# Seven products that nobody reads in the opening of a two-layer hybrid encoder

## The reference

```python
for l in range(DEPTH):
    mod = c_act @ w_ada[l] + b_ada[l]
    x = _layer(x, mod, ...)
...
shift, scale, gate = jnp.split(mod, 3, axis=-1)
h = _rmsnorm(x, norm_w) * (1.0 + scale[:, None]) + shift[:, None]
proj = h @ w_in
```

## Time and profile before

| what | before |
|---|---|
| median of 3 runs | 1139.76 us (1139.59 to 1139.95) |
| the profiled execution | 1139.91 us |
| its span, first to last instruction | 1138.2 us |
| mean granted TensorE clock in the span | 0.993 |
| TensorE busy | 1116.9 us, 98% of the span |
| DVE, ACT, POOL busy | 666.4, 529.3, 569.4 us |

### The profile page before, as it was taken

The page is one execution under the profiler, slowest core; times in us unless marked ns, Lnnn a source line. Parts: engine busy times, 40 slices in busy tenths (PEclk is TensorE's granted clock), DMA queues, the critical chain, the costliest instruction groups (busy, mean ns, idle before and its releaser), DMA issues.

```text
span 1138.2 us, 15271 instructions
## 1 busy us (share of the span) xinstructions
PE 1116.9 (98%) x5843; PEld 920.5 (81%) x5843; DVE 666.4 (59%) x824; ACT 529.3 (47%) x924; POOL 569.4 (50%) x411
## 2 busy tenths in 40 slices
PE   6999999999999999999999999999999999999997
PEld 5778888888888888888898788888788887788885
DVE  4716466579887555538870635665988854131365
ACT  5544266655445524224462535656545453232234
POOL 5536444445535545545814363444445535454455
PEclk8999999999999999999999999999999999999998
DMA  9656423235443456653304463224433523443332
GB/s 322 205 131 204 126 80 88 76 110 139 121 117 73 135 172 199 211 152 104 99 20 102 144 200 93 75 75 120 120 111 94 139 64 84 111 139 93 101 104 93
DMA packets 203482, 140.80 MB, mean 124 GB/s; under 512 B 12001, under 2 KB 191249, under 8 KB 203409
## 3 DMA queue, kind: packets, MB, share of 16 engines
q1 hardware_dynamic: 202632, 138.91, 42.3%
q10 hardware_dynamic: 776, 0.91, 0.3%
HBM read 136.64 MB, written 2.63 MB: 122 GB/s over the span
## 4 chain that ended last, share of the span: by engine, by line
PE 91%; POOL 3%; DVE 2%; SPq 1%; DMA 1%; ACT 1%; issue 0%; DVEq 0%; POOLq 0%
PE main L679 74%; PE psC L679 6%; PE psA L679 5%; PE psB L679 4%; POOL w_lo L597 3%; SPq L395 1%; DMA big<-in_w_ada 1%; PE psB L912 1%; PE psB L892 1%; DVE h_lo L1540 1%; SPq L423 0%; ACT w_hi L1092 0%; DVE psC L1493 0%; DVE tmp L1535 0%; PE psC L921 0%
## 5 line engine op out<-in xcount | busy, mean ns | idle before, releaser
L597 POOL TENSOR_TENSOR w_lo<-raw,w_hi 128x512 fp32r<-128x512 f32 x344 | 510.1, 1504 | 535.6 <-ACT w_hi L1092 535.4
L679 PE MATMUL main<-h_hi,w_hi 128*128 128x512 f32 x976 | 390.4, 401 | 3.8 <-ACT h_hi L1092 2.9
L679 PE MATMUL main<-h_hi,w_lo 128*128 128x512 f32 x976 | 380.0, 390 | 0.0
L679 PE MATMUL main<-h_lo,w_hi 128*128 128x512 f32 x976 | 379.5, 390 | 0.0
L1092 ACT ACTIVATE w_hi<-raw 128x512 fp32r<-128x512 f32 x344 | 200.0, 623 | 309.7 <-PE main L679 174.4
L679 PEld LDWEIGHTS main<-h_hi,w_hi 128*128 128x128 f32 x976 | 183.6, 188 | 52.1 <-issue 11.6
L679 PEld LDWEIGHTS main<-h_hi,w_lo 128*128 128x128 f32 x976 | 183.2, 188 | 39.2
L679 PEld LDWEIGHTS main<-h_lo,w_hi 128*128 128x128 f32 x976 | 183.4, 188 | 37.7 <-issue 1.9
L1855 DVE TENSOR_TENSOR tmp<-main,misc 128x512 f32<-128x512 f32 x32 | 22.1, 691 | 165.6 <-PE main L679 163.1
L1701 DVE SCALAR_TENSOR_TENSOR misc<-main,cols,misc 128x511 f32<-128x511 f32 (+2 forms) x96 | 71.9, 749 | 61.0 <-ACT misc L1092 58.4
L679 PE MATMUL main<-y_hi,w_hi 128*128 128x512 f32 x256 | 100.6, 393 | 0.0
(11 more groups left out here) (282 smaller groups left out, 1418.0 us busy)
## 6 DMA issues: line engine op xcount, KB each, us to landing
raw<-in_w_in SPq DMA_DIRECT2D x124, 512.0 KB, 3.9
xbc<-in_w_ada SPq DMA_DIRECT2D x16, 512.0 KB, 4.8
zs<-in_w_ada SPq DMA_DIRECT2D x16, 512.0 KB, 4.6
raw<-in_w_pc SPq DMA_DIRECT2D x16, 512.0 KB, 3.8
raw<-in_w_out SPq DMA_DIRECT2D x16, 512.0 KB, 3.6
zs<-in_w_ada SPq DMA_DIRECT2D x16, 256.0 KB, 7.7
xbc<-in_w_in SPq DMA_DIRECT2D x8, 512.0 KB, 7.4
big<-in_w_ada SPq DMA_DIRECT2D x16, 256.0 KB, 7.2
```

Source lines behind the costliest of these rows:

```text
L597: nc.gpsimd.tensor_tensor(lo_b[:, cut, :], raw_b[:, cut, :], hi_b[:, cut, :].bitcast(F32), ALU.subtract).then_inc(s_split[b], 2 * BT_ // kt)
L679: return nc.tensor.matmul(o, a, b_, start=start, stop=stop)
```

## The change

Seven products are added to TensorE's stream in the opening. Each multiplies the identity (128x128, fp32) with 256 columns of the transposed rows, and writes columns 512 to 767 of `psB`, where nobody reads them. Three stand between `spread` and the first sums, four between these sums and `wide_pair(0)`. The wait for ACT's copies moves ahead of the first three.

```diff
             spread(psC0, rms, 1)
+
+            def unread(n):
+
+                for _ in range(n):
+                    mm(psB[:, 512:768], ident[:, :], stage_x[:, 0, 0:256])
+
+            pe.wait_ge(s_xca, 2)
+            unread(3)
             quarter_sums(0)
             pe.wait_ge(s_cols, 1)
             pe.wait_ge(s_xc, 2)
-            pe.wait_ge(s_xca, 2)
+            unread(4)
             for q in range(QUARTERS - 1):
                 wide_pair(q)
```

## The result

The changed kernel takes 1141.5 us (median of 21 runs, 1140.61 to 1142.72), the kernel before 1139.75 us (21 runs, 1139.41 to 1140.46). The ratio is 1.0015 with a 95% interval of [1.0009, 1.0022]: 1.75 us slower, which is under 0.2% and clear of zero. It lies within the forecast range, close to its upper end (1141.6), and twice as far from the kernel before as the 0.8 us that I gave.

The account below looks back on a forecast made before the run. DVE was taken to bound the opening, so TensorE's 2.9 us gain brings 0; slow sums of quarter 1 add 0.8 us to the median 1139.76, giving 1140.6, stated as 1140.5. The range was 1139.4 to 1141.6.

Parts of the forecast that it names:

- What bounds the opening: Up to `wide_end`: slab transfers of quarter 1, then DVE set the end, with about 0.1 us to spare over TensorE.
- the 2.9 us of TensorE: First sums and `wide_pair(0)`: full clock frees 0.8 and 2.1 us on TensorE, but gains 0 on the path.
- The clock of the start: Opening: clock 1.00 up to 15.8, then 1.2 GHz until 26.05; first transposes, 0.21 us each, taken at about half speed.
- Price of the products: Added products of 256 columns: 0.45 us each, 1.35 for three and 1.8 for four, twice that at 1.2 GHz.
- Two pauses of 1.8 us: TensorE waits 1.8 us ahead of block 0's low rows and 1.8 more ahead of the sums of quarter 1.
- The clock falls in the pauses: Ahead of the sums of quarter 1: they take 1.87 us, not 1.05, making DVE and all behind it 0.8 late.
- a term that I had put at 0: Low clock reaching beyond the start of `wide_pair(1)`: costs half its length less 0.1 us; likeliest 0.
- Sum: Whole kernel: 0 if the clock holds at 30.9, +0.8 us if not, added to the median 1139.76.
- Faster: Rival in the opening: TensorE, not DVE, holds it and the 2.9 us come through, 1136.9; chance 0.02.
- no effect: Rival in the opening: clock holds at 30.9 or falls where it did, everything covered, 1139.7 to 1139.9; chance 0.37.
- products too long: Rival around the first sums: clock stays low all through, up to +1.1 us, 1140.9; chance 0.06.
- Slower by more than 0.2%: Rival at `wide_pair(1)`: low clock for 4.4 us costs 2.2, slow sums 0.8 more, up to 1142.7; chance 0.07.

Follow-up runs that it names:

- exchanged kernels: One weight load issued ahead of a `w_ada` slab instead of behind it: kernel before 1139.29 us, changed kernel 1139.49, with only the four later unread products 1139.46.
- six zero products: Kernel before plus six products of zero weights directly ahead of `wide_end`, order of loads as before: 1143.32 us, 3.12 +- 0.18 over the kernel before.
- second trace: The changed kernel run again with nothing altered: median 1141.74 us, ratio 1.0015 to the kernel before; the traced execution took 1142.97 us.
- filled kernels: Changed kernel plus three zero-weight products ahead of the sums of quarter 1: 1141.71 us; the same with the weight load ahead of the slab: 1141.03 us.

## Why the prediction was right, and where it was short

The number was right in part by luck. The range held the result only because it left 1 us for a low stretch; the slice that I thought likeliest, 1140.2 to 1141.2, didn't. And by the exchanged kernels the larger part of the loss comes from a load that the prediction doesn't mention.

- *What bounds the opening, and that the 2.9 us of TensorE go nowhere.* Right, within 0.3 us. `wide_pair(0)` ran at full clock, and no kernel with unread products had a lower median than the kernel before with the same order of loads. Among the exchanged kernels, the fastest run of the changed one was 0.2 us below the fastest of the kernel before. The link to TensorE that I didn't see is POOL: where TensorE was early, POOL made its `y_lo` earlier, and DVE's two `h_lo` took 2.21 us and not 2.50.
- *The clock of the start.* I read 1.00 up to 15.8, and in the same breath took the first transposes for half speed. Their rows say the latter: the first two groups of eight start 1.76 and 1.71 us apart, 0.21 for each product, for 0.13 in the third with its drain, though PEclk is 1.00 over all of it. So the 1.00 of PEclk up to about 9 us doesn't agree with the products there. The sum doesn't hang on it.
- *Price of the products.* Right, if a little high: eight records took 1.97 us with the drain at full clock, and six zero products moved the next start by 2.40, 0.40 for a product where I took 0.45. As `wide_end` came only 2.17 later apart from the first transfers, TensorE had 0.2 us to spare and not 0.1. The first three took 2.56 from start to start of the next, at half speed, for the 2.4 that follow from the 0.35 and 2.0 given. The first sums were 0.8 late at their start, not 0.45, but the clock came back within them (1.21 for 1.87), so they ended as before.
- *Two pauses of 1.8 us.* Right in kind, not in size: 0.45 and 1.44 where the clock was low for the first three, 1.98 and 0.24 (the sums then slow) where it was not.
- *The clock falls in the pauses and costs 0.8 us in the sums of quarter 1.* Half right. A fall goes with the long pauses, but in no trace does it come in them: it came 0.9 to 2.3 us behind their end. In the second trace that is soon enough for slow sums, 1.86 us, as predicted; `wide_end` is then 1.67 us late and not 0.8. In the first the sums are fast, and TensorE is late into `wide_pair(1)`: 0.85 us, so the 0.8 of the sum was met there by a term that I had put at 0. I had set the low stretch beyond the start of `wide_pair(1)` to 0; it reached 0.7 us past it in the one trace and 0.9 in the other (35.77 to about 36.6).
- *The step that failed* is the *Sum*: it ended at `wide_end`, as if all behind it moved by as much ("DVE, and all behind it, is 0.8 us late"). Behind it stands a load of weights that was barely in time, and it added 0.75 and 1.52 us in the two traces. By the exchanged kernels it is the larger part, some 1.3 of 1.7 us; what they leave for the term that I did sum up is 0.40 +- 0.42 us.
- *The rivals.* "Faster" fell, "no effect" and "products too long" too. "Slower by more than 0.2%" did not come in the median, but single runs passed it (up to 1142.72 and 1143.36 us in the two sets). The one of them that was traced, 1142.97 us, did so by the opening and the load together and not by the clock alone.

What stays open is, first, how often the clock falls in each kernel, since each has one trace (the changed kernel two), and why the filled kernels are slow in most runs. Second, why the load takes 5.1 to 5.2 us in some traces and 5.8 to 6.8 in others, from its issue to ACT's start. It is longer with a later opening in most of them: 5.2 for loads issued at 97.45 and 97.60, 6.8 at 99.26. But it took 5.07 at 98.25, in the kernel before with two added products, and 6.67 at 98.14. Something in its way doesn't move with the engines, and none of the views shown here says what.

## What to carry to other kernels

Work that nobody reads, put into a wait to keep TensorE's clock up, can pay only if a faster TensorE lets the path end earlier. Where another engine sets the pace, it moves the idle further down the stream, and the clock may fall behind it, perhaps in a stretch that has nothing to spare. So look for the next pause behind the one that is filled, and for what is late if the clock falls in it. And a shift at the head of a long program is not worth its own size only: a transfer that was just in time further on can add to it (3.12 us for 2.29 with the six zero products). The queue order that caused it, a load of weights behind a slab that waits for DVE, was worth 0.66 +- 0.24 us by itself, without any change to the opening; the kernel before with that exchange has the lowest median here.

## What the runs showed of the hardware that I had not expected

- The moment at which the clock first falls differs between executions: 15.85 in the kernel before, about 14.0 with the load exchanged, 16.2 with six products ahead of `wide_end`, all with the same work up to there. So it doesn't need the idle ahead of the first sums: at 14.0 TensorE was in its one-column products (12.74 to 15.18 in that trace), and in the changed kernel, at 15.4, it was still in `spread`. The return moved too (26.05, 27.6, 26.4). The Trainium skill (TensorE: Matmul & The Clock Gate, "Part 1: The HAM clock gate") says that the point at which the clock rises varies from run to run, by about half a microsecond either way; the traces agree that it varies, and show the three returns up to 1.5 us apart. One trace is thus one draw: the two traces of the changed kernel have the low stretches in different places.
- A higher mean clock is no sign of a faster run. The filled kernel took 1142.97 us in a run with a mean clock of 0.998, and the kernel before 1139.58 with 0.994.
- A load of 512 KB, issued 0.4 us behind a slab of 512 KB, took between 5.1 and 6.8 us from its issue until ACT could start on it, with the same transfers around it.
- The same DVE instruction (`h_lo`, 128x512) took 0.74 us by itself and 1.54 to 1.78 us where it ran beside POOL's `y_lo`; which of the two `h_lo` it was followed when POOL came to it.
